# VectorE copies the second head's turned weights, ScalarE the first head's, in both softmax attentions

## What is computed

```python
# first block, in each of 2 layers; per block of 128 queries
s = (einsum('bqhd,bkhd->bhqk', qn, k_nope) + einsum('bqhd,bkd->bhqk', qr, k_rope)) * scale
s = where(kpos[None, :] <= qpos[:, None], s, -inf)
pr = softmax(s, axis=-1)
out = einsum('bhqk,bkhd->bqhd', pr, v)
...
# second block; per block of 128 queries, top-k keys shared by the 8 heads
logits = einsum('bqhd,bqkhd->bhqk', qb, kg) * HEAD_DIM ** -0.5 + bias
p = softmax(where(valid, logits, -inf), axis=-1)
out = einsum('bhqk,bqkhd->bqhd', p, vg)
```

## Time and profile before

| | |
|---|---|
| median of 3 runs | 3663.06 us (3661.84 to 3667.1) |
| the profiled execution's own time | 3663.07 us |
| its span | 3661.2 us |
| mean granted TensorE clock | 0.975 of full speed |
| TensorE (PE) busy | 3492.2 us, 95% of the span |
| VectorE (DVE) busy | 1753.0 us, 48% |
| ScalarE (ACT) busy | 1229.8 us, 34% |
| GpSimd (POOL) busy | 468.3 us, 13% |

### The profile page before, as it was taken

How to read it: one execution, slowest core, us unless ns; L and a number is a source line. 1 busy time by engine, 2 the same in 40 slices (tenths; PEclk the granted TensorE clock), 3 DMA queues, 4 the chain that set the end, 5 groups by cost and what they waited for, 6 DMA issues and landing times. The chain is left out here.

```text
span 3661.2 us, 46927 instructions
## 1 busy us (share of the span) xinstructions
PE 3492.2 (95%) x19692; PEld 2738.9 (75%) x19692; DVE 1753.0 (48%) x2177; ACT 1229.8 (34%) x1796; POOL 468.3 (13%) x399
## 2 busy tenths in 40 slices
PE   8999999889999899999989899998999989889998
PEld 7888676777888678886758678876788857668886
DVE  5543475546532555324845565324433248653323
ACT  3222435233222422224352332224422244643221
POOL 0002113440002000031134300030000100300001
PEclk9999999999999999999999899999999999999999
DMA  5432220014432244322200144321322222113231
GB/s 186 138 119 91 70 69 31 3 48 143 138 114 89 76 147 139 106 86 70 69 19 4 64 138 138 109 87 65 121 97 97 89 71 75 47 55 101 98 99 63
DMA packets 88442, 326.58 MB, mean 89 GB/s; under 512 B 12672, under 2 KB 12672, under 8 KB 88104
## 3 DMA queue, kind: packets, MB, share of 16 engines
q1 hardware_dynamic: 88232, 323.57, 27.5%
HBM read 321.15 MB, written 4.74 MB: 89 GB/s over the span
## 5 line engine op out<-in xcount | busy, mean ns | idle before, releaser
L227 DVE TENSOR_TENSOR w_low<-w_raw,w_high 128x1024 fp32r<-128x1024 f32 (+1 forms) x481 | 635.6, 1322 | 1252.6 <-ACT w_high L219 1251.7
L219 ACT ACTIVATE w_high<-w_raw 128x1024 fp32r<-128x1024 f32 (+1 forms) x481 | 538.8, 1121 | 1307.0 <-PE ffa_ps L245 434.3
L243 PE MATMUL ffa_ps<-ffa_x_high,w_high 128*128 128x512 f32 x704 | 282.8, 402 | 14.0 <-DVE ffa_x_low L307 14.0
L243 PE MATMUL b_f_ps<-b_f_x_high,w_high 128*128 128x512 f32 x704 | 280.1, 398 | 11.8 <-DVE b_f_x_low L446 11.8
L244 PE MATMUL ffa_ps<-ffa_x_low,w_high 128*128 128x512 f32 x704 | 281.3, 400 | 0.0
L245 PE MATMUL ffa_ps<-ffa_x_high,w_low 128*128 128x512 f32 x704 | 279.8, 397 | 0.0
L244 PE MATMUL b_f_ps<-b_f_x_low,w_high 128*128 128x512 f32 x704 | 279.3, 397 | 0.0
L245 PE MATMUL b_f_ps<-b_f_x_high,w_low 128*128 128x512 f32 x704 | 279.0, 396 | 0.0
L243 PE MATMUL mix_proj_ps<-mix_x_high,w_high 128*128 128x512 f32 x416 | 171.0, 411 | 12.4 <-DVE mix_x_low L386 12.3
L243 PEld LDWEIGHTS ffa_ps<-ffa_x_high,w_high 128*128 128x128 f32 x704 | 133.5, 190 | 47.0 <-DVE w_low L227 8.1
L243 PEld LDWEIGHTS b_f_ps<-b_f_x_high,w_high 128*128 128x128 f32 x704 | 133.3, 189 | 47.1 <-issue 12.4
(11 more groups left out here) (552 smaller groups left out, 7097.5 us busy)
## 6 DMA issues: line engine op xcount, KB each, us to landing
w_raw<-in_ffa_in SPq DMA_DIRECT2D x88, 512.0 KB, 3.5
w_raw<-in_ffb_in SPq DMA_DIRECT2D x88, 512.0 KB, 3.5
w_raw<-in_ffn_in SPq DMA_DIRECT2D x88, 512.0 KB, 3.5
w_raw<-in_mix_in SPq DMA_DIRECT2D x77, 512.0 KB, 3.5
w_raw<-in_ffa_out SPq DMA_DIRECT2D x32, 704.0 KB, 4.1
w_raw<-in_ffb_out SPq DMA_DIRECT2D x32, 704.0 KB, 4.1
w_raw<-in_ffn_out SPq DMA_DIRECT2D x32, 704.0 KB, 4.1
ffa_ada_raw<-in_w_ada SPq DMA_DIRECT2D x36, 512.0 KB, 4.3
```

The costliest lines, as they stand in the source:

```text
L219: act.activation(self.high[:, self.place(n, 0, kt)], self.raw[:, n % SLOTS, :kt * P], ACT.Copy).then_inc(self.rounded, 1)
L227: dve.tensor_tensor(self.low[:, whole], self.raw[:, n % SLOTS, :kt * P], self.high[:, whole].bitcast(F32), ALU.subtract).then_inc(self.spl ...
L243: pe.matmul(out, w_high, x_high[:, k0 + k, :], start=start and place == 0, stop=False)
```

## The change

VectorE copies head 1's turned weights, ScalarE only head 0's. VectorE's copy stands in its step `n` behind the inverse of unit `n - 1`, and waits until both heads of unit `n - 3` are turned. The one semaphore `pt_ready` becomes two, one for each copying engine; the turn of head `a` waits for that head's own semaphore, and `weigh` waits for both. In all 16 + 2 x 8 = 32 copies change engine.

```diff
@@ names
-    names = ["scored", "dve_step", "added_ready", "max_ready", "exp_ready", "sum_inverted", "diag_ready", "turned", "pt_ready",
-             "o_done", "o_taken"]
+    names = ["scored", "dve_step", "added_ready", "max_ready", "exp_ready", "sum_inverted", "diag_ready", "turned",
+             "pt_ready_act", "pt_ready_dve", "o_done", "o_taken"]
@@ turn(self, pe, n)
-            at_least(pe, self.pt_ready, 2 * (n - 1) + a + 1)
+            at_least(pe, self.pt_ready[a], n)
@@ weigh(self, pe, n)
-        pe.wait_ge(self.pt_ready, 2 * (n + 1))
+        for copied in self.pt_ready:
+            pe.wait_ge(copied, n + 1)
@@ vector(self, dve, n, own)
             dve.reciprocal(self.inverse[:, slot, :], self.total[:, slot, :]).then_inc(self.inverted, 1)
+        if 0 <= n - self.LAG < self.count:
+            k = n - self.LAG
+            dve.wait_ge(self.turned, 2 * k + 2)
+            at_least(dve, self.o_done, k - 1)
+            dve.tensor_copy(self.pt[:, k % 2, 1, 0:self.width(k)], self.pr[1][:, 0:self.width(k)]).then_inc(self.pt_ready[1], 1)
@@ scalar(self, act, n)
-            for a in range(2):
-                act.wait_ge(self.turned, 2 * k + a + 1)
-                at_least(act, self.o_done, k - 1)
-                act.activation(self.pt[:, k % 2, a, 0:self.width(k)], self.pr[a][:, 0:self.width(k)], ACT.Copy)\
-                    .then_inc(self.pt_ready, 1)
+            act.wait_ge(self.turned, 2 * k + 1)
+            at_least(act, self.o_done, k - 1)
+            act.activation(self.pt[:, k % 2, 0, 0:self.width(k)], self.pr[0][:, 0:self.width(k)], ACT.Copy)\
+                .then_inc(self.pt_ready[0], 1)
```

More of the change, by code:

```diff
@@ L2087, in signals @@
         (self.scored, self.dve_step, self.added_ready, self.max_ready, self.exp_ready, self.inverted, self.diag_ready,
-         self.turned, self.pt_ready, self.o_done, self.o_taken) = sems
+         self.turned, *self.pt_ready, self.o_done, self.o_taken) = sems
     def width(self, n):
```

## The result

The changed kernel took 3676.01 us, the median of 11 runs, against 3667.37 us for the kernel before, also the median of 11 runs: a ratio of 1.0023, with a 95% interval from 1.0015 to 1.0031, or 5.5 to 11.4 us of loss. Forecast were 6.4 us of loss, 0.17%, which lies in both intervals; the time forecast, 3669.5 us, and its upper end of 3674.5 were too low.

A forecast was written before the change was run, and what follows sets the result against it. TensorE, busy all 11.00 us of the sparse attention's period, was the bound. Losses of 4.4 + 0.2 + 1.5 there and 0.3 in the latent attentions made +6.4 us on 3663.06: 3669.5 us, range 3663.5 to 3674.5.

The forecast's parts named there:

- ScalarE's relief: Sparse attention's steady period: one ScalarE copy a unit less, 0.592 us at 512 columns, worth nothing since TensorE never idles.
- The copies on VectorE: 32 added copies out of PSUM, priced 0.683 us at 512 columns; as busy time they fit, 10.3 of 11 us.
- The wait in front of the mask: Sparse attention: VectorE masks a unit only after an earlier turn; TensorE stalls 2.2 us before scores of 9 and 13.
- the small units: Sparse attention's units with shorter masks or near ties: 0.2 us in all, including ScalarE's later head 0 copy.
- The third stall: End of sparse attention, last unit 15: score of 15 to turn of 13 grows from 7.25 to 8.74, +1.5 us.
- The latent attentions: Both latent attentions: 2.8 us of VectorE delay falls into 2.7 of slack, about 0.15 us lost each, 0.3 together.
- Separate semaphores: TensorE's waits in all three stages: same events counted by another counter, costing nothing.
- A: Rival, chance 0.13: sparse attention's stall is absorbed by hidden slack; loss under 2 us, 3663 to 3665.
- B: Rival, chance 0.06: less ScalarE work shortens TensorE's waits for its copies; up to 4.8 us faster, 3658.3.
- C: Rival, chance 0.12: GpSimd's long products hold VectorE's copies in the sparse attention; some +10 us, 3673.
- mask at 3142.32: Sparse attention: a VectorE mask reading PSUM took its plain 0.69 us amid GpSimd's 6.32, evidence against copies being held.
- D: Rival, chance 0.08: idle TensorE is granted 1.2 GHz again in the sparse attention; +18 us over two periods, 3681.

The follow-up runs named there:

- copy_later: Changed kernel with VectorE's copy one step later, behind the next unit's shift, so no mask waits for a turn; 3666.86 us, ratio 0.9996 to the kernel before.
- sparse_only: Changed kernel, but ScalarE keeps both copies in the latent attentions, so the move acts in the sparse attention alone; 3675.38 us, ratio 1.0014 to the kernel before.
- latent_only: Changed kernel, but ScalarE keeps both copies in the sparse attention, so the move acts in the two latent attentions alone; 3668.42 us, ratio 0.9998.

## Why the prediction was right about the change, and wrong about the time

**ScalarE's relief is worth nothing.** Right: ScalarE went from 10.19 to 8.80 us in a period and the period grew; copy_later, with the same relief and no wait, keeps 11.01 us.

**The copies on VectorE, 0.683 us at 512 columns.** Right: 0.692 in the mean, 0.56, 0.43 and 0.28 at 384, 256 and 128.

**The wait in front of the mask.** Shown, by adding it alone, by moving the copy to a place where it finds the turn done, and by doubling what stands behind it: periods of 12.67, 11.01 and 14.35 us beside 13.27. The forecast was 13.2. Its make-up was a little different. The chain is 4.93 us, not 5.01, and TensorE is done with the weigh of 7 at 3180.93 + 1.09 = 3182.02, 3.28 us behind the turn's end: 2.93 of work (2.82 forecast) and 0.35 of a wait of its own, before the turn of 8, for ScalarE's late copy. So the stall at the score is 1.65 and not 2.2. The period grew by 2.27 us. Of these, 1.65 and 0.35 are waits, and the other 0.27 are lost because instructions at a wait overlap less (the turn of 9 starts 0.83 us behind the score of 13 that has waited; in copy_later, without the wait, 0.64). The 0.2 us that the forecast took for the small units and ScalarE's later copy was the right kind of term, and too small.

**The third stall.** 1.6 us for 1.5, and 0.16 more behind it (3205.34 - 3197.77 = 7.57 us against 7.41 in the kernel before), the last weighs of 2.04 us for 1.85. The relief of 0.15 us that the forecast took off for ScalarE's copy did not come: from the end of the exponentials (3196.70 + 0.19 = 3196.89) to the turn (3197.77) it is 0.88 us, and was 0.89.

**The latent attentions.** 0.24 and 0.23 us for 0.15, near in size, but by luck, for the mechanism was another. The forecast had VectorE's delay reach the exponentials of 7 and so the turns behind them; from the first score to the start of the last weighs the first attention takes 645.34 - 612.95 = 32.39 us, and took 32.34. The other 0.19 us are in the last weighs, and copy_later, which has no wait there in front of VectorE's work, keeps them (34.39 us).

**Separate semaphores.** Not nothing, but small. sparse_only's latent attentions, which have the new counters and both copies on ScalarE, take 34.29 and 34.28 us, where those of the kernel before took 34.19 to 34.21 in four profiles. The difference is in the last weighs again, 1.94 us, and latent_only has the same 1.94 at the end of its sparse attention:

```profile
642.01 1.94 PE L2112 MATMUL mix_ma_o<-mix_ma_pt,mix_vm 128*64 128x128 f32 x28
```

So about half of the 0.19 us comes with the counters, the other half with VectorE's copy.

**The rivals.** A falls: the stall is not absorbed. B falls by the period. C falls by the copies beside GpSimd, none of them held; the forecast's "mask at 3142.32" was a fair witness for them. D was half seen. The clock did fall, in three of four executions, but for about two units and 1.56 us, and not for two periods and 18 us. Which stalls bring it about stays open. Its counter-argument, the latent attention that kept 1.00 at the same busy share, did not hold: the wait there is 1.56 to 1.59 us, with no fall behind it, and the new one 1.64, with a fall in three of four.

**What failed: the base.** The measured 3676.01 us lie above the range of 3663.5 to 3674.5. The step was "it stands 0.01 us from the median of the runs; a change in the span can be added to the median as it is". The profile stood near the median of three runs, but both lay at the low end of what the kernel before takes: the eight further runs of the first comparison have a median of 3669.87 us, the three before it 3663.06. The kernel before had medians of 3667.37, 3669.32 and 3670.94 us in the three comparisons, and single runs from 3660.99 to 3678.47; its first profile is the one of four with a fast opening (by 3.0 to 3.6 us), an early rise (0.75) and a short way (1.70). From a base of 3667 to 3671 the same sum gives 3674 to 3677. The loss was sized rightly (6.8 us in the three stages at equal clock), and the time and its range were not, because the range held only the scatter of the change's own terms and none of the base's. Of the 6.5 us between 3669.5 and 3676.01, 4.3 are the base (3667.37 for 3663.06); the other 2.2 are the loss of that comparison, 8.6 for 6.4, in which the fall of the clock may have had a part. How often it came in those runs is not known, so that rest stays open.

No version run here is faster than the kernel before: copy_later is level with it.

## What to carry to other kernels

Moving an operation to an engine that executes in order moves its wait too, and what is queued behind it is then as late as the thing waited for. Here it did not help that VectorE was busy only 7.60 of 11 us, because the wait stood in front of the mask of the next long unit; one place later the same work cost 0.2 us. Before adding a forecast difference to a median, look at how far single runs of the base scatter, and put that into the range of the time, while the size of the difference is judged by itself.

## What was not expected of the hardware

One program, no change: the same opening products took 21.8 to 22.0 us at a granted clock of 1.00 and 24.8 to 25.5 at 0.66 to 0.83, and the way to the output projection 11.8 or 13.5. With the 0.75 us of the stage these make some 6 us. The runs of the kernel before scatter over more, 3660.99 to 3678.47 us on one chip, and where the rest lies was not looked for.

And a stall can cost more than its length. Behind 1.64 to 1.65 us of idle TensorE the clock fell in three of four executions of the changed kernel (1.56 us more), behind 2.32 us in the doubled copy's first latent attention too (3.0 us more), and behind 2.70 at the end of its sparse attention (1.55 more). But it did not fall behind 1.65 us before the score of 9 in the same executions of the changed kernel, nor behind 2.08 us before the turn of 13 in its first, nor behind 2.14 before the score of 13 with the doubled copy. What decides between these was not settled.
